# Modulation rows: four column groups that each finish a quarter of the columns, and one matmul to turn a row

## What is computed

```python
# layers A and B, i = 0, 1: w_ada[i] is 1024 x 3072
shift,   scale,   gate   = split(silu(c)     @ w_ada[i] + b_ada[i], 3)   # tokens
shift_c, scale_c, gate_c = split(silu(c_ctx) @ w_ada[i] + b_ada[i], 3)   # context
u  = h  * (1 + scale)   + shift
uc = hc * (1 + scale_c) + shift_c
y, yc = mixer(u, uc, ...)
h  = layer_norm(ALPHA * h  + gate   * y)
# third layer: w_mod is 1024 x 6144
sh1, sc1, gt1, sh2, sc2, gt2 = split(silu(c_2) @ w_mod + b_mod, 6)
h1 = rms_norm(x) * (1 + sc1) + sh1   # ... attention and convolution, then experts
```

## Time and profile before

| | |
|---|---|
| time, median of 3 runs | 1220.15 us (1218.71 to 1221.67) |
| the profiled execution, first to last instruction | 1220.9 us |
| TensorE busy | 96% |
| VectorE busy | 45% |
| ScalarE busy | 25% |
| mean granted TensorE clock | 0.981 of full |
| read from HBM | 309.40 MB |

### The profile page before, as it was taken

How to read it: one execution, slowest core, us unless ns; L and a number is a source line. 1 busy time by engine, 2 the same in 40 slices (tenths; PEclk the granted TensorE clock), 3 DMA queues, 4 the chain that set the end, 5 groups by cost and what they waited for, 6 DMA issues and landing times.

```text
span 1220.9 us, 15705 instructions
## 1 busy us (share of the span) xinstructions
PE 1169.4 (96%) x6224; PEld 728.7 (60%) x6224; DVE 546.1 (45%) x1278; ACT 303.1 (25%) x705; POOL 23.0 (2%) x33
## 2 busy tenths in 40 slices
PE   4999999989999999999999898999999999999996
PEld 2476876658778888568885586444444444444442
DVE  3253339987566330882799533122222222222223
ACT  0000128971240001670612333111111111111112
POOL 0000000000000001110000000000000000000000
PEclk9999999999999999999999698999999999999998
DMA  9851219014343225456375594999999999999991
GB/s 341 312 207 69 70 51 364 2 35 172 126 153 125 81 70 181 117 180 219 138 275 194 209 315 187 417 426 427 428 428 427 428 428 429 428 429 428 428 417 42
DMA packets 82327, 311.42 MB, mean 255 GB/s; under 512 B 18129, under 2 KB 19228, under 8 KB 69466
## 3 DMA queue, kind: packets, MB, share of 16 engines
q1 hardware_dynamic: 78672, 309.56, 65.1%
q10 hardware_dynamic: 3386, 0.86, 0.3%
q0 software_dynamic: 208, 0.17, 0.1%
HBM read 309.40 MB, written 1.18 MB: 254 GB/s over the span
## 4 chain that ended last, share of the span: by engine, by line
PE 84%; DVE 10%; DMA 2%; ACT 2%; issue 1%; SPq 1%; DVEq 0%; ACTq 0%
PE ps L1238 18%; PE ps L883 17%; PE ps L1270 9%; PE ps L1204 5%; PE ps L984 5%; PE ps L1216 5%; DVE G L2141 4%; PE ps L934 3%; PE ps L948 3%; PE ps L733 3%; PE ps L832 3%; PE ps L921 2%; PE ps L1088 2%; PE ps L1064 2%; DMA ring<-in_a_w_in 2%; PE ps L745 1%
## 5 line engine op out<-in xcount | busy, mean ns | idle before, releaser
L1238 PE MATMUL ps<-ring,prob 128*64 128x512 f32 x704 | 188.1, 592 | 1.2 <-issue 1.2
L1238 PEld LDWEIGHTS ps<-ring,prob 128*64 128x64 f32 x704 | 61.8, 137 | 100.3 <-issue 100.3
L2306 DVE TENSOR_TENSOR prob<-ps,prob 128x512 f32<-128x512 f32 x16 | 17.2, 1077 | 193.7 <-PE ps L1238 193.7
L1270 PE MATMUL ps<-ring,prob 128*64 128x512 f32 x352 | 78.0, 595 | 0.0
L883 PE MATMUL ps<-U,ring 128*128 128x256 f32 x304 | 69.8, 380 | 1.3 <-DVE Q L1986 1.3
L1238 PE MATMUL ps<-K,prob 128*64 128x512 f32 x160 | 70.3, 592 | 0.0
L1204 PEld LDWEIGHTS ps<-bias,U 128*128 128x128 f32 x512 | 60.8, 198 | 13.4 <-issue 13.4
L1382 ACT ACTIVATE prob<-ps,soft 128x512 f32<-128x512 f32 (+2 forms) x112 | 64.3, 593 | 9.6 <-DVE soft L1824 7.6
L1204 PE MATMUL ps<-bias,U 128*128 128x128 f32 x512 | 63.8, 285 | 1.1 <-DVE bias L2267 1.1
L2314 DVE TENSOR_TENSOR probT<-ps,cst 128x512 f32<-128x512 f32 x32 | 22.1, 692 | 94.6 <-PE ps L1270 94.6
L883 PEld LDWEIGHTS ps<-U,ring 128*128 128x128 f32 x304 | 57.5, 190 | 9.4 <-DVE Q L1986 1.7
(11 more groups left out here) (376 smaller groups left out, 1849.8 us busy)
## 6 DMA issues: line engine op xcount, KB each, us to landing
ring<-in_w_exp_gate SPq DMA_DIRECT2D x22, 2048.0 KB, 17.9
ring<-in_w_exp_up SPq DMA_DIRECT2D x20, 2048.0 KB, 16.6
ring<-in_w_exp_down SPq DMA_DIRECT2D x20, 2048.0 KB, 19.6
ring<-in_w_ada SPq DMA_DIRECT2D x12, 2048.0 KB, 16.2
ring<-in_w_mod SPq DMA_DIRECT2D x12, 2048.0 KB, 9.0
ring<-in_b_w_in SPq DMA_DIRECT2D x8, 2048.0 KB, 8.7
ring<-in_a_w_in SPq DMA_DIRECT2D x5, 2048.0 KB, 18.8
ring<-in_w_in SPq DMA_DIRECT2D x5, 2048.0 KB, 10.0
```

The costliest lines, as they stand in the source:

```text
L1238: last = mm(ps[x * CAP:(x + 1) * CAP, 2 + i, :], xg[:, k, x * CAP:(x + 1) * CAP], chunk(n, 2 * i + x, turn)[0][:, k, :], start=(k == 0), s ...
L1270: last = mm(ps[x * CAP:(x + 1) * CAP, 5 + c, :], hidT[:, k, x * CAP:(x + 1) * CAP], chunk(n, 4 + x, turn)[0][:, k, c * 512:(c + 1) * 512], ...
```

## The change

`stream` now divides the columns over the groups instead of the inputs: group `t` makes columns 128t to 128t+127 over all eight input blocks. That is 32 matmuls of 128 columns in place of eight of 512, and each group holds complete sums. The block that ACT copies is 128x128 instead of 128x512. `fold` becomes one matmul: the row is the stationary operand, and the moving one is picked out of the identity matrix, the columns 32t+v for the four groups t and the vectors v, four or eight columns; nothing is added any more. Chunks 4 and 5 of `mod_b` (`spread`) keep the old form. 22 chunks change.

```diff
+        def spread(stage, c):
+            return stage == "mod_b" and c >= 4
...
                 n = PLACE[stage][c]
                 landed(n)
-                for i in range(2):
-                    for t in range(4):
-                        k = 2 * t + i
-                        last = mm(ps[32 * t:32 * t + 32, bank, :], sil[:, k, :], slot(n)[:, k, :],
-                                  start=(i == 0), stop=(i == 1))
+                if spread(stage, c):
+                    for i in range(2):
+                        for t in range(4):
+                            k = 2 * t + i
+                            last = mm(ps[32 * t:32 * t + 32, bank, :], sil[:, k, :], slot(n)[:, k, :],
+                                      start=(i == 0), stop=(i == 1))
+                else:
+                    for k in range(KT):
+                        for t in range(4):
+                            last = mm(ps[32 * t:32 * t + 32, bank, 0:P], sil[:, k, :],
+                                      slot(n)[:, k, t * P:(t + 1) * P], start=(k == 0), stop=(k == KT - 1))
                 last.then_inc(st[stage], 1)
...
-                for m in range(4):
-                    col = (S if stage != "ada0" and c < 4 else 0) + (4 * place + m) * nv
-                    part = row[:, m // 2, (m % 2) * P:(m % 2 + 1) * P] if len(row.shape) == 3 else row[:, m * P:(m + 1) * P]
-                    last = mm(ps[:, bank, col:col + nv], part,
-                              cs("fold")[:, v0:v0 + nv], start=True, stop=True)
-                last.then_inc(col_done, 1)
+                col = (S if stage != "ada0" and c < 4 else 0) + 4 * place * nv
+                mm(ps[:, bank, col:col + 4 * nv].rearrange("p (t v) -> p t v", t=4), row,
+                   ident.rearrange("p (t r) -> p t r", t=4)[:, :, v0:v0 + nv], start=True, stop=True
+                   ).then_inc(col_done, 1)
...
-                    src = ps[:, banks[c % len(banks)], :]
-                    if len(row.shape) == 3:
-                        src = src.rearrange("p (i t) -> p i t", i=2)
-                    a(row, src, ACT.Copy).then_inc(row_ok, 1)
+                    a(row, ps[:, banks[c % len(banks)], 0:row.shape[1]], ACT.Copy).then_inc(row_ok, 1)
```

More of the change, by code:

```diff
@@ L334, in build @@
         rows_beside = {"ada1": K[:, 3072:4096].rearrange("p (b n) -> p b n", b=2),
-                       "mod_a": U[:, :].rearrange("p (b i t) -> p b i t", b=4, i=2)[:, 0:2, :, S:T],
+                       "mod_a": U[:, :].rearrange("p (b t) -> p b t", b=KT)[:, 0:2, S:T],
                        "mod_b": U[:, 2048:3584].rearrange("p (b n) -> p b n", b=3)}
+        def spread(stage, c):
+            return stage == "mod_b" and c >= 4
         def modrow(stage, c):
             if c < EARLY.get(stage, 0):
-                return rows_beside[stage][:, c]
+                return rows_beside[stage][:, c, 0:P]
             if stage == "ada0" and c >= 4:
-                return rows_gate0[:, c - 4, :]
-            return rows_after[:, c % 2, :]
+                return rows_gate0[:, c - 4, 0:P]
+            return rows_after[:, c % 2, 0:COLS if spread(stage, c) else P]
         route = probT[:, :].rearrange("p (r n) -> p r n", n=2 * 32)
```

## The result

| | before | changed |
|---|---|---|
| time, median of 7 runs each | 1221.54 us (1218.71 to 1227.85) | 1213.29 us (1208.94 to 1214.37) |
| ratio, 95% interval | | 0.9918 (0.9898 to 0.9937) |
| the profiled execution, first to last instruction | 1220.9 us | 1207.3 us |
| its mean granted TensorE clock | 0.981 | 0.986 |

The changed kernel is faster. The forecast, 1210.1 us, is 3.2 us under the median that came, and the range of 1205.5 to 1218.5 holds it. The medians differ by 8.3 us; the ratio, worked out on 1221.5 us, says 10.0 us, between 7.7 and 12.5. The two profiled executions differ by more, 13.6 us. Part of that is not the change, as the clock will show.

What follows compares the result with a forecast made beforehand. TensorE was taken as the bound (96% busy, 84% of the chain that ended last). The terms sum to -10.0 us, taking the profiled 1220.9 to 1210.9; the median forecast is 1210.1 us, range 1205.5 to 1218.5.

Steps and rivals of the forecast that it cites:

- The new stream: In each changed chunk: 16 waves of four matmuls, 0.109 us a wave, 1.88 us a stream, +0.03 us a chunk.
- rival 2: Stream records can't issue fast enough: 0.216 us a wave, 1239.8 us; quotes about 62 or 25 ns a matmul; chance 9%.
- `ada0` 2 and 3: Both folds are on the path, the second through VectorE, for whose first modulated tile TensorE waits: -1.3 us.
- the first two pairs: `ada0` 4 and 5, `ada1` 2 and 3: two streams and two folds without a gap, -0.97 us each.
- `ada1` 5: TensorE sits waiting for the row, so fold and copy both count: -0.67 - 0.3 = -1.0 us.
- `mod_a` 2 and 3: Third place with two streams and two folds without a gap; copy 0.29, passing on 0.1: -0.97 us.
- Attention A: Folds of `ada1` 0 and 1 end 1.3 us earlier; VectorE makes good only its 0.81 us wait: -0.8 us.
- Attention B: Folds of `mod_a` 0 and 1: only VectorE's 0.37 us wait counts, -0.4 us; -1.3 if TensorE bounds there.
- `mod_a` 4 and 5: Hidden behind VectorE's convolution, for which TensorE still waits 1.02 us at 668.48: 0.
- rival 3: Gains are absorbed: VectorE and ScalarE bound all three attentions, only TensorE-bound places count, -5.8, 1214.4 us; chance 11%.
- `mod_b` 0 to 2: Folds at the third attention's start: VectorE loses its two waits of 1.66 and 1.48 us, no more: -3.0 us.
- `mod_b` 3: The fold stands ahead of the sum for which ScalarE waits 0.55 us: -0.6 us.

Runs made afterwards that it cites:

- fine64: Changed kernel with each stream cut into 64-column matmuls, 256 records a stream; 1241.15 us, ratio 1.0154 to the kernel before.
- again: Changed kernel, unedited, rerun as yardstick of the first follow-up set; 1211.35 us, ratio 0.9909 to the kernel before.
- again_3: Changed kernel, unedited, rerun as yardstick of the third follow-up set; 1211.33 us, ratio 0.9910 to the kernel before.
- again_2: Changed kernel, unedited, rerun as yardstick of the second follow-up set; 1213.10 us, ratio 0.9921 to the kernel before.
- four_all: Changed kernel with every fold back to four matmuls, new stream and narrow copy kept; 1221.74 us, ratio 0.9998 to the kernel before.
- four_pairs: Changed kernel with four-matmul folds only at `ada0` 4 and 5, `ada1` 2 and 3, `mod_a` 2 and 3; 1211.41 us, ratio 0.9908 to the kernel before.
- four_modb: Changed kernel with four-matmul folds only at `mod_b` 0 to 2; 1215.26 us, ratio 0.9948 to the kernel before.

## Why the prediction was right, and where its terms were off

The mechanism held: the stream at equal cost, the fold cheaper, and the gain only at the places that bound. Step by step:

- **The new stream.** Predicted 0.109 us a wave and 1.88 us a stream, measured 0.109 and 1.89. The choice between 0.109 and 0.216 was made by the nearest rows, the products with two groups and 128 columns. The doubt was the lasting rate of records, 14 ns; fine64 shows eight records in 56 ns, so the rate was far from its limit, and both prices a matmul that rival 2 quotes are too high for matmuls of different column groups, which start every 14 ns there. The earlier trace rows had already the larger of them against it: 16 matmuls at 0.109 us for two are one in 55 ns.
- **The fold and the copy.** Predicted -0.67 us a fold; it takes 0.22 to 0.24 in place of 0.90. Copy predicted 0.29, measured 0.27 to 0.28.
- **`ada0` 2 and 3, and the first two pairs.** -1.39, -1.04 and -1.04, predicted -1.3 and -0.97 each.
- **`ada1` 5.** -0.85, predicted -1.0: the fold gives 0.67, the copy 0.2 and not 0.3.
- **The second pair's remainder.** 0.50 us of it went to a new wait, 0.34 us at 272.23 for VectorE's sums (L1706). The term took for granted that VectorE was ahead there; nothing was late before, and the row that shows it comes only with the change.
- **`mod_a` 2 and 3.** -0.63 in place of -0.97. The copy's 0.1 "passing on" was taken as constant. ScalarE here issues loads while the streams run (ACTq is its queue's own rows), the last of them took 1.56 us where it took 0.35 before, and it comes to the copies late:

```profile
540.82 2.17 ACTq L1470 DMA_DIRECT2D bias<-in_b_router_group  x1
543.30 1.56 ACTq L1471 DMA_DIRECT2D bias<-in_b_router_expert  x1
544.90 0.45 ACT L1340 ACTIVATE prob<-ps 128x128 f32<-128x128 f32 x2 [4.63 <-PE ps L743]
```

```profile
545.24 0.61 PE L753 MATMUL ps<-cst,prob 128*128 128x4 f32 x4 [0.58 <-ACT prob L1340]
```

  The streams' first row was complete at about 542.8, half way; both rows are copied at 544.90. In again and again_3 the wait isn't there, in again_2 it is (0.56 us).
- **Attention A.** -0.88, predicted -0.8: VectorE's wait of 0.81 us is gone, and that of 0.38, which stands behind the streams, is still there with 0.44 at 179.70. The reading was right.
- **Attention B: the term that was mis-sized most.** Predicted -0.4, measured -1.33, and kept to 544 us. The prediction put the gain at VectorE's one wait, 0.37 us at 505.05. That wait was short because VectorE was late itself: its two L1845 took 1.44 us from 500.12, and 0.88 from 503.60, while GpSimd worked beside it. Before:

```profile
500.02 0.86 POOL L664 TENSOR_TENSOR bias<-bias,cst 128x384 f32<-128x384 f32 x1 [26.12 <-DMA bias<-relpad]
```

```profile
500.12 1.44 DVE L1845 TENSOR_SCALAR prob<-prob,soft 128x512 f32<-128x512 f32 x2
...
503.60 0.88 DVE L1845 TENSOR_SCALAR prob<-prob,soft 128x512 f32<-128x512 f32 x2
```

  four_all has the same folds as before, and its two operations there take 0.88 us; its wait is 0.93 us:

```profile
502.13 0.88 DVE L1856 TENSOR_SCALAR prob<-prob,soft 128x512 f32<-128x512 f32 x2
502.93 0.28 DVE L1867 TENSOR_TENSOR U<-ps,Q 128x128 f32<-128x128 f32 x1
504.15 0.77 DVE L1900 TENSOR_TENSOR ps<-ps,bias 128x256 f32<-128x256 f32 x2 [0.93 <-PE ps L935]
```

  The two folds are worth 1.34 us, and VectorE's slack there, with the 0.56 us that its slow pair of operations had taken, is 0.93 us or more. In the changed kernel VectorE has no gap from 491.45 to 535.84. The alternative of the prediction, "-1.3 if TensorE bounds", gave the right number; that VectorE's 0.56 us of slowness is the reason for the difference wasn't tried by itself. The traces support it: eight have the single fold there, and all are 1.3 us earlier right behind the two folds. Six keep that to the attention's end, with 0 to 0.25 us by which VectorE's operations of this line are longer than usual in the attention; again_3, with 0.73 us, keeps 0.88, and four_pairs, with 0.56 us, keeps 1.06. So what the folds bring here depends on how often the two engines meet in an execution.
- **The stall, +1.00.** Missing from the prediction. It looked for the price of more records in the rate of issue and not in their supply. In the changed kernel it costs 0.3 to 1.2 us; with twice the records it turned a gain into a loss.
- **`mod_a` 4 and 5, costed at 0.** Their folds and copies did bring 1.60 us by 618.53, and all of it was gone at the start of the third attention: TensorE now waits 1.10 and 1.38 us for the softmax there, behind VectorE's convolution, where it waited 1.02 before. What was won before 554 us stayed (-8.50, then -8.48), since VectorE's work had moved forward with it. This is what rival 3 supposed for all attentions, true at one place.

```profile
658.13 0.49 PE L929 MATMUL ps<-K 64*128 64x128 f32 x4 [1.10 <-ACT prob L1387]
660.00 0.44 PE L942 MATMUL ps<-cst,prob 128*128 128x128 f32 x2 [1.38 <-DVE prob L1850]
```

- **`mod_b` 0 to 2.** -3.8, predicted -3.0, the sum of VectorE's two waits. four_modb gives 3.8 at the place, 2.6 of it left at 685 us, and 3.9 in the time (2.6 at equal clock). The term lies inside these; whether it was read too small stays open, since the half clock lies over different instructions of this attention in every execution.
- **`mod_b` 3.** -0.78, predicted -0.6. The single fold brings 0.67 on TensorE (0.92 before, 0.25 now, start to next), so TensorE and not ScalarE's wait of 0.55 us set it.
- **The sum.** Without the 3.3 us of clock the profiled execution is 10.5 us earlier at its end, the timed runs say 10.0 (7.7 to 12.5), and the prediction said 10.0. At equal clock the three sets give 10.1, 10.2 and 10.7. That the total is so near is partly luck: by this pair of traces attention B and `mod_b` 0 to 3 were too small by 0.9 and 1.0 us, against 1.0 us for the stall, 0.5 for the new wait at 272.23 and 0.3 at `mod_a` 2 and 3, none of them foreseen. The stream, the single fold, the copy and the gains in `ada0` and attention A came out by their reasons.

## What to carry to other kernels

To cost a smaller tile of a matmul, take the pace from the nearest row with that many moving columns and several column groups. A matmul that moves few columns costs its weight load (0.112 us a record here for one or two columns, and no more for eight), so count loads, not columns. A gain behind a wait of another engine is worth that engine's slack; before reading the slack from one gap, look whether the engine's own operations ahead of the gap ran at their usual length. Before calling two versions equal, look at the clock that their runs were granted.

## What the runs showed of the hardware that was not expected

- Instructions can run short. TensorE's come in packets of 16 KB, 256 records each, a packet 0.9 to 1.7 us long, and a stalled stream went on 1.3 to 1.6 us after one had landed. With 128 records of both kinds in 1.89 us the stream stalled at one place of the program for 0.27 to 1.24 us; with 256 in that time it stalled seven times for 1.6 to 4.4 us; with 32 or 64 it never did. Records added ahead of it, 18 or 24 matmuls with their loads, took the stall away; four_all, with more still, has one of 2.33 us at another place.
- Matmuls of different column groups start 7 ns apart, and eight records in 56 ns last for a whole stream of 64-column waves.
- Two VectorE operations (128x512) that take 0.88 us took 1.44 while a GpSimd operation of 0.86 ran beside the first; in four_all the same two took 0.88 where they did not meet one, and 1.59 at 506.28 us, with a GpSimd operation from 506.33.
- The half-clock stretches are not fixed to the program. The same kernel had one at 29.8 us in one execution and none there in three others, and the mean clock of its first seven timed runs went from 0.980 to 0.988, some 4 to 5 us of time.
